# Routed expert blocks in groups of four: one pass of each engine's loop holds four blocks in place of two

## The reference

```python
    flat_e = top_idx.reshape(-1).astype(jnp.int32)          # 2048 tokens x 8 experts of 64
    counts = jnp.bincount(flat_e, length=N_EXPERTS).astype(jnp.int32)
    padded = (counts + MOE_BLOCK - 1) // MOE_BLOCK * MOE_BLOCK     # MOE_BLOCK = 128
    ...
    def block_fn(args):
        tok, w, e = args
        return swiglu(x_pad[tok], we_gate[e], we_up[e], we_down[e]) * w[:, None]
    ...
    out = jnp.zeros((n_tok + 1, d), hf.dtype).at[row_tok].add(ys.reshape(n_rows, d))
```

## Time and profile before

| | |
|---|---|
| Median of 3 runs | 2932.33 us (2926.17 to 2951.27) |
| Profiled execution, its own time | 2938.84 us |
| Its span in the trace | 2937.1 us |
| PE, DVE, ACT, POOL busy | 89%, 53%, 39%, 50% of the span |
| Granted clock of PE, mean | 0.951 |
| DMA | 534.62 MB, mean 182 GB/s |

### The profile page before, as it was taken

One profiled execution on the slowest core, in us unless ns is written; L12 is line 12 of the kernel. 1 busy time (PEld: TensorE's weight loads), 2 busy tenths in 40 slices (PEclk: granted clock), 3 DMA queues, 4 the chain that ended last, 5 costly groups with the idle time before them and its releaser, 6 DMA issues.

```text
span 2937.1 us, 49464 instructions
## 1 busy us (share of the span) xinstructions
PE 2620.7 (89%) x11395; PEld 1888.8 (64%) x11396; DVE 1571.1 (53%) x2558; ACT 1145.9 (39%) x1534; POOL 1471.7 (50%) x1756
## 2 busy tenths in 40 slices
PE   6999998975889999589999999999999999999980
PEld 2755553512456666367877787788777787877860
DVE  6389987981456656333333344335444455545535
ACT  5133212213222232134444444445555555555532
POOL 2012215214366666144555555656767776777656
PEclk9999999987889999799999999999999999999995
DMA  8162405533322231367777777787988888998977
GB/s 263 61 130 96 162 1 90 200 125 140 115 72 94 101 100 59 138 185 188 189 200 194 193 193 214 210 233 218 271 261 264 256 262 261 278 278 240 272 210 264
DMA packets 305610, 534.62 MB, mean 182 GB/s; under 512 B 39254, under 2 KB 205142, under 8 KB 304778
## 3 DMA queue, kind: packets, MB, share of 16 engines
q1 hardware_dynamic: 251770, 355.93, 36.8%
q0 software_dynamic: 51472, 173.70, 24.9%
q10 hardware_dynamic: 2304, 4.20, 0.4%
HBM read 395.76 MB, written 138.01 MB: 182 GB/s over the span
## 4 chain that ended last, share of the span: by engine, by line
PE 51%; issue 19%; POOL 11%; DVE 9%; POOLq 7%; ACT 2%; DMA 1%; SPq 1%; DVEq 0%; ACTq 0%
PE psm L1109 25%; PE psm L1056 8%; DVE arena L1754 6%; PE psm L954 5%; PE psm L915 4%; POOL arena L2149 3%; POOL arena L2146 2%; PE psm L1102 2%; POOL st L2139 2%; POOLq L2145 2%; POOLq L2167 2%; PE psm L854 1%; PE psm L1046 1%; POOLq L2166 1%; POOLq L2158 1%
## 5 line engine op out<-in xcount | busy, mean ns | idle before, releaser
L1109 PE MATMUL psm<-whi,xhi 128*128 (+1 forms) x1424 | 576.9, 405 | 56.3 <-issue 27.0
L1109 PE MATMUL psm<-whi,xlo 128*128 (+1 forms) x1424 | 559.5, 393 | 0.0
L1109 PE MATMUL psm<-wlo,xhi 128*128 (+1 forms) x1424 | 557.9, 392 | 0.0
L1905 DVE TENSOR_TENSOR arena<-psm,arena 128x256 f32<-128x256 f32 x178 | 75.5, 424 | 644.8 <-ACT arena L1453 644.8
L1109 PEld LDWEIGHTS psm<-whi,xhi 128*128 128x128 f32 x1424 | 269.2, 189 | 129.6 <-issue 60.5
L2154 POOL TENSOR_TENSOR wlo<-raw,whi (+1 forms) x64 | 330.5, 5164 | 42.5 <-ACT whi L1482 42.5
L1754 DVE SCALAR_TENSOR_TENSOR arena<-arena,cw 128x1024 f32<-128x1024 f32 x240 | 335.7, 1399 | 8.6
L1109 PE MATMUL psm<-whi,hhi 128*128 (+1 forms) x712 | 295.7, 415 | 42.2 <-issue 22.7
L1109 PEld LDWEIGHTS psm<-whi,xlo 128*128 128x128 f32 x1424 | 269.1, 189 | 59.2
L2163 POOL DMA_INDIRECT acc_d<-arena x162 | 277.3, 1712 | 57.7 <-issue 53.0
L1109 PEld LDWEIGHTS psm<-wlo,xhi 128*128 128x128 f32 x1424 | 269.9, 190 | 51.5
(11 more groups left out here) (353 smaller groups left out, 3986.3 us busy)
## 6 DMA issues: line engine op xcount, KB each, us to landing
raw<-in_we_gate_dram SPq DMA_DIRECT2D x64, 1024.0 KB, 8.4
raw<-in_we_up_dram SPq DMA_DIRECT2D x64, 1024.0 KB, 11.9
raw<-in_we_down_dram SPq DMA_DIRECT2D x64, 1024.0 KB, 5.1
arena<-in_w_ada_dram SPq DMA_DIRECT2D x12, 2048.0 KB
arena<-in_x_dram SPq DMA_DIRECT2D x32, 512.0 KB, 5.4
h_d<-arena SPq DMA_DIRECT2D x17, 512.0 KB, 2.7
acc_d<-arena SPq DMA_DIRECT2D x17, 512.0 KB, 4.3
arena<-in_w_in_dram SPq DMA_DIRECT2D x16, 512.0 KB, 6.1
```

The costliest lines, as they stand in the source:

```text
L1109: m = TE.matmul(o, a, w, start=(n == 0), stop=(n == len(todo) - 1))
```

## The change

On PE, ACT and POOL one pass of the loop holds four steps in place of two, written out by a Python loop; the buffer number still alternates. On DVE the first step is taken out of the loop, and a pass holds four in place of one. So that the loops come out even after the first step and before the tail, the count of blocks is rounded up to two more than a multiple of four: DVE adds one, shifts right by two, multiplies by four and adds two. The bound `NB` grows from 192 to 194, and the tables' length `NROW` from 194 to 200. SP's stream is as before.

```diff
-NB += NB % 2
-NROW = NB + 2
+NB += (2 - NB) % 4
+NROW = NB + 6
...
@@ PE
-            with pe.Fori(NT + 2, nb + NT, 2) as b:
-                routed_step(b, 0)
-                routed_step(b + 1, 1)
+            with pe.Fori(NT + 2, nb + NT, 4) as b:
+                for n in range(4):
+                    routed_step(b + n, n % 2)
...
@@ ACT
-            with act.Fori(NT + 2, nb + NT, 2) as b:
-                routed_step(b, 0)
-                routed_step(b + 1, 1)
+            with act.Fori(NT + 2, nb + NT, 4) as b:
+                for n in range(4):
+                    routed_step(b + n, n % 2)
...
@@ DVE, count_blocks
-                do(ts(nbi, nbi, 1, None, ALU.arith_shift_right), V.tensor_tensor_scan(ids, ones64, ones64, 0.0, ALU.mult, ALU.add))
-                do(ts(nbi, nbi, 2.0, None, ALU.mult), ts(twice_m, cntf[:, E - 1:E], 2.0, -1.0, ALU.mult, ALU.add))
+                do(ts(nbi, nbi, 2, None, ALU.arith_shift_right), V.tensor_tensor_scan(ids, ones64, ones64, 0.0, ALU.mult, ALU.add))
+                do(ts(nbi, nbi, 4.0, 2.0, ALU.mult, ALU.add), ts(twice_m, cntf[:, E - 1:E], 2.0, -1.0, ALU.mult, ALU.add))
...
@@ DVE, routed blocks
-            with dve.Fori(NT + 1, nb + NT) as b:
-                routed_step(b)
+            routed_step(NT + 1)
+            with dve.Fori(NT + 2, nb + NT, 4) as b:
+                for n in range(4):
+                    routed_step(b + n)
...
@@ POOL
-            with pool.Fori(NT + 2, nb + NT, 2) as b:
-                step(b, 0)
-                step(b + 1, 1)
+            with pool.Fori(NT + 2, nb + NT, 4) as b:
+                for n in range(4):
+                    step(b + n, n % 2)
```

## The result

The changed kernel is slower: 2955.69 us (median of 20 runs, 2943.8 to 2967.85) beside 2933.86 us for the kernel before on the same chip (20 runs, 2924.43 to 2962.43). The ratio is 1.0063, with a 95% interval of 1.0042 to 1.0083: about 18 us lost by the ratio (the two medians lie 22 us apart), where 13 us were forecast as gained, and the time lies above the range.

What follows compares the result with a forecast made beforehand. PE was taken to bound the routed blocks (busy 1355.99 of 1400 us). Saved branches, 15.6 us, less 2.9 us taken back gave 12.7, say 13 us: median 2932.33 to 2919 us, range 2898 to 2952 us.

Steps and rivals of the forecast that it cites:

- the term for ACT, DVE and POOL: Loops of these three engines: fewer branches, costed at nothing beyond POOL's small give-back, since their waits for PE cover them.
- the half of 2.2 us above: Between 2640 and 2790 us, POOL's own lost edges may return half of the 2.2 us PE would lose there.
- PE's edges: PE's loop branches: 40 of 80 go, 25 saving 0.30 us and 15 saving 0.54 us, together 15.6 us.
- The "issue" wait: Sign: PE's wait for its own sequencer before the gate-up matmuls would fall by 12 to 17 us.
- What is taken back: PE's waits for POOL's split, 1.8 us, and ACT's copy waiting for POOL, 1.1 us: 2.9 us off the gain.
- All of it taken back: Rival: scatter chain holds PE after 2090 us, so only the first half's 20 edges count; 2925 to 2932 us, chance 0.14.
- Code: Instruction fetch: PE's loop grows from 264 to 524 instructions and still fits, costed at nothing.
- Blocks: Count of routed blocks: old and new rounding both give 162, no block added, 0 us.
- The rival on the slower side: PE's longer loop no longer fits and is fetched again at each back edge: 56 to 164 us, 3027 us, chance 0.08.

Runs made afterwards that it cites:

- again: The kernel before, unchanged, run once more for a second profile; 2964.44 us in its single run.
- act4: The kernel before with only ACT's loop holding four steps and the block count by the new rule; ratio 1.0005 to the kernel before.
- dve4: The kernel before with DVE's part of the change alone: first step taken out, four steps a pass; ratio 1.0008 to the kernel before.
- yfirst2: The kernel before with POOL's wait for ACT's copy moved ahead of the index copy; ratio 0.9978 to the kernel before.
- pool4: The kernel before with only POOL's loop holding four steps; ratio 1.0077 to the kernel before.
- f2: The kernel before with POOL's loop variable shifted by one, adding one register instruction in the first step of a pass; ratio 1.0084 to the kernel before.
- swap2: The kernel before with POOL's two waits ahead of the hold in the other order, ACT's copy first; ratio 1.0089 to the kernel before.
- lean2: The kernel before with POOL's register load, index copy and hold put ahead of the wait for the landing, and a second index buffer; ratio 1.0012.
- pe4: The full change with ACT, DVE and POOL left as before, so only PE's loop holds four steps; ratio 0.9984 to the kernel before.
- f4: The full change with POOL's loop variable shifted by two, moving one register instruction to another step of the pass; ratio 0.9981 to the kernel before.
- no_pool: The full change with POOL's old loop of two steps; ratio 0.9983 to the kernel before.
- lean4: The full change with POOL's register load, index copy and hold put ahead of the wait for the landing, and a second index buffer; ratio 0.9969.
- yfirst4: The full change with POOL's wait for ACT's copy moved ahead of the index copy; ratio 0.9943 to the kernel before.
- swap4: The full change with POOL's two waits ahead of the hold in the other order, ACT's copy first; ratio 1.0058 to the kernel before.
- thinf2: f2 with most of the gate and up weight transfers left out from the third expert on; ratio 0.9899 to the kernel before.

## Why the prediction was wrong

**The step that failed** is the term for ACT, DVE and POOL, "I cost this at nothing but the half of 2.2 us above", for POOL. It counted what the change takes from POOL's stream (branches) and not what it puts in. The change put the long form of a wait into 40 more of the 162 steps, and among them into all the fourth blocks without slack; B shows +15 us for the change, +17 to +27 for the other kernels with it. The added register instructions stand in POOL's compiled stream before anything runs; the forecast had looked at PE's and DVE's streams only. Cover was argued from ACT's wait for PE; but POOL waits for landings, a chain that ACT's slack does not cover, and the rows that show POOL holding ACT's copy and PE's split were used for 2.9 us only.

**PE's edges** agree with the forecast, as far as profiles can tell. Over the profiles with two steps a pass A is 786.0 us in the mean (nine of them: before, again, act4, dve4, yfirst2, pool4, f2, swap2, lean2), over those with four 777.8 (eight). That is 8.2 us for 20 edges in A, 0.41 each; the forecast had 15.6 / 40 = 0.39. A scatters by 5 to 6 us within each group, so the difference is uncertain by some 5 us, and that the two figures agree so closely is luck. The step of the timeline with an edge took 0.25 us more than the one without. The "issue" wait fell by 10.7 us at the matmul (12 to 17 were forecast) and did not fall at the weight load. A single pair of profiles misleads here too: before against the change alone gives 17.

**What is taken back** was mis-sized. 2.9 us were taken off, 1.8 us of that for a longer wait for POOL's split, which grew by 15.1 us in the change; and even without POOL's long form the second half gave nothing that these profiles show. Among kernels with C at 0.74 and an unchanged chain B is 585.3 us in the mean with two steps (five) and 587.4 with four (four). That is the rival "All of it taken back": only the first half's 20 edges, about 8 us, count. pe4, f4 and no_pool, with 5 to 6 us gained, fit it, though each of their intervals takes in no change. Its "against", that only 15 copies were held by POOL, did not hold: a count of waits before the change does not show what holds PE once it is faster. That POOL's chain is what holds it there is argued from lean4 over lean2, not shown.

**Code** was right: no refetch, in a loop of 524 instructions on PE.

**Blocks** were right: 162.

**The rival on the slower side** was the wrong one. A fetch of instructions stood at 0.08, and none said that the unrolled code puts a wait in another place. The change is slower by 0.6%, which lies within 1%; what the forecast misses is the range, by 4 us, and the sign. (A slip without weight: 26 us more than 2919 would be 2893, not 2895.)

**The sum does not close.** The three kernels with four steps on PE and the long form have B at 602.0 us in the mean, 16.7 above the five with two steps and the short form; less 8.2 us gained in A, that is 8 to 9 us lost, and 18 were measured (12 to 24 by the interval). In the first pair of profiles A gave 17 us, B cost 15, and the stretch from block 143 to 161 cost another 15 (195.0 after 180.2). This stretch scatters by 20 us between two profiles of one kernel, so what is left of the loss cannot be put in a place. f2 is alike: 25 us lost, 17 of them in B.

**Also open:** why yfirst4 gains 17 us when f4 and no_pool gain 5 to 6. Their B and C are the same; its A is the lowest of all (768.8 us), but one profile's A scatters by 10 us and more, and the intervals of the ratios overlap (0.9918 to 0.9969, 0.9957 to 1.0004).

## What to carry over

Unrolling changes which loop values are a plain register, and so where the compiler puts register instructions and which of two waits the sequencer sits out; compare the streams of every engine, most of all the one in a chain of DMA landings, before calling its part free. Directly before an instruction that needs the engine's own last result, wait for that result alone, and put the other waits ahead of the instruction that makes it. A chain that costs nothing visible before the change can still have no slack: here a loss of 0.41 us in it showed at once, and two to four times over.

## What the runs showed of the hardware

- From release to scatter POOL takes 0.74 us if the hold carries the wait for the index copy, and 1.13 to 1.15 us if a sequencer instruction of 17 or 35 ns does: 0.4 us for the place of a wait.
- Of two waits written directly one behind the other ahead of the hold, the hold carried the first and the sequencer sat out the second, in either order (the kernel before, swap2, swap4).
- PE ran a loop of 524 instructions 40 times with no instruction packet behind the first pass.
- POOL's 128 x 1 add took 0.19 us alone and 1.10 us at one place under DVE's split; POOL's scatter instruction took 1.61 us alone and 2.40 us in the median when it started under one.
- The scatters of the fourth blocks landed 7.1 us after their start in the median where the weights' transfer was issued 1.54 us after that start (at scatter 95), and 8.6 us where it was issued 1.13 us after it. thinf2 has the long form with less of that traffic, and its chain showed no loss.
